# First in-projection and the memory's keys and values as three products of split parts, residual loaded a second time

## The reference, cut to what matters

```python
h  = rmsnorm(x, norm_attn)
z  = h @ w_in                       # 2048 -> some 4200 columns, read by four mixers
o  = concat(mla(z), fox(z), nsa(z), swa(z))
x  = x + group_rmsnorm(o) @ w_out
...
m  = rmsnorm(mem, mem_norm)
k, v = m @ w_xk, m @ w_xv           # 2048 -> 2048 each, used in the second block
```

## Time and profile before

| | before |
|---|---|
| median of 3 runs | 3607.71 us (3600.49 to 3613.07) |
| the profiled execution, its own time | 3600.61 us |
| its span in the trace | 3598.5 us |
| PE busy | 3231.2 us, 90% |
| PEld busy | 2423.2 us |
| DVE busy | 1803.0 us |
| ACT busy | 1125.7 us |
| mean granted clock | 0.970 |
| the first stage (to the first product of `w_out`) | 0 to 700.5 us of the span |

### The profile page before, as it was taken

One profiled execution on the slowest core, in us unless ns is written; L12 is line 12 of the kernel. 1 busy time (PEld: TensorE's weight loads), 2 busy tenths in 40 slices (PEclk: granted clock), 3 DMA queues, 4 the chain that ended last, 5 costly groups with the idle time before them and its releaser, 6 DMA issues.

```text
span 3598.5 us, 41404 instructions
## 1 busy us (share of the span) xinstructions
PE 3231.2 (90%) x17284; PEld 2423.2 (67%) x17284; DVE 1803.0 (50%) x2793; ACT 1125.7 (31%) x2177; POOL 306.2 (9%) x284
## 2 busy tenths in 40 slices
PE   7999999899999999979998899898998768777776
PEld 6667875599999999978897899644443223232222
DVE  1212122265555555665666646555555556655554
ACT  1212122235343434346554434222222222222221
POOL 0000000000000000000000000122222212221221
PEclk9989899999999999989998999999999999999999
DMA  6433433345555555534444434799999999999997
GB/s 188 158 112 111 148 119 118 120 164 176 181 183 187 178 186 183 180 135 161 156 154 175 153 129 141 318 428 427 427 428 421 428 428 424 428 428 428 429 428 339
DMA packets 98946, 908.76 MB, mean 253 GB/s; under 512 B 10278, under 2 KB 20902, under 8 KB 23624
## 3 DMA queue, kind: packets, MB, share of 16 engines
q0 software_dynamic: 36864, 536.89, 35.1%
q1 hardware_dynamic: 49140, 347.05, 27.4%
q10 hardware_dynamic: 12756, 22.18, 2.2%
HBM read 896.64 MB, written 9.44 MB: 252 GB/s over the span
## 4 chain that ended last, share of the span: by engine, by line
PE 68%; DMA 21%; DVE 6%; ACT 3%; issue 1%; ACTq 0%; DVEq 0%; SPq 0%; POOL 0%; POOLq 0%
PE sums L742 12%; PE sums L743 12%; PE sums L744 12%; DMA area<-in_uv,cst 12%; PE sums L938 9%; PE sums L474 8%; DMA hT<-in_uv,cst 5%; PE sums L493 5%; DMA ringx<-in_uv,cst 3%; PE sums L894 2%; DVE area L1964 1%; PE sums L455 1%; ACT cst L987 1%; PE sums L530 1%; ACT area L987 1%
## 5 line engine op out<-in xcount | busy, mean ns | idle before, releaser
L742 PE MATMUL sums<-xh,wh 128*128 128x256 f32 x2688 | 776.7, 289 | 48.6 <-DVE xl L1720 20.4
L1689 DVE TENSOR_TENSOR wl<-ring,wh 128x1024 fp32r<-128x1024 f32 x480 | 585.2, 1224 | 436.0 <-ACT wh L987 435.1
L743 PE MATMUL sums<-xl,wh 128*128 128x256 f32 x2688 | 766.2, 285 | 0.0
L744 PE MATMUL sums<-xh,wl 128*128 128x256 f32 x2688 | 766.0, 285 | 0.0
L987 ACT ACTIVATE wh<-ring 128x1024 fp32r<-128x1024 f32 x480 | 505.7, 1056 | 507.1 <-PE sums L744 495.4
L742 PEld LDWEIGHTS sums<-xh,wh 128*128 128x128 f32 x2688 | 520.4, 194 | 58.2 <-issue 44.3
L938 PE MATMUL sums<-area,cst 128*128 128x512 f32 x984 | 459.5, 613 | 103.5 <-ACT cst L987 103.3
L743 PEld LDWEIGHTS sums<-xl,wh 128*128 128x128 f32 x2688 | 521.0, 194 | 0.8
L744 PEld LDWEIGHTS sums<-xh,wl 128*128 128x128 f32 x2688 | 520.7, 194 | 0.0
L987 ACT ACTIVATE cst<-cst 128x1 f32<-128x1 f32 (+2 forms) x786 | 234.1, 299 | 914.6 <-DVE cst L1964 852.3
L938 PEld LDWEIGHTS sums<-area,cst 128*128 128x128 f32 x984 | 183.3, 193 | 362.1 <-issue 191.5
(11 more groups left out here) (263 smaller groups left out, 3477.0 us busy)
## 6 DMA issues: line engine op xcount, KB each, us to landing
ring<-in_w_up SPq DMA_DIRECT2D x64, 1024.0 KB, 4.8
ring<-in_w_down SPq DMA_DIRECT2D x64, 1024.0 KB, 4.8
ring<-in_w_in_a SPq DMA_DIRECT2D x53, 1024.0 KB, 4.9
ring<-in_w_out SPq DMA_DIRECT2D x32, 1024.0 KB, 4.8
ring<-in_w_xq SPq DMA_DIRECT2D x16, 1024.0 KB, 4.8
ring<-in_w_xo SPq DMA_DIRECT2D x16, 1024.0 KB, 4.8
ring<-in_w_pq SPq DMA_DIRECT2D x16, 1024.0 KB, 11.4
ringx<-in_w_in_a SPq DMA_DIRECT2D x13, 1024.0 KB, 4.9
```

What stands on the lines that cost most here:

```text
L742: te.matmul(bank[:, 0:T], wh[:, j % 3, x], hi[:, k, :], start=k == 0, stop=False)
L743: te.matmul(bank[:, 0:T], wh[:, j % 3, x], lo[:, k, :], start=False, stop=False)
L744: mm = te.matmul(bank[:, 0:T], wl[:, j % 3, x], hi[:, k, :], start=False, stop=k == 15)
L1689: ve.tensor_tensor(wl[:, j % 3, :], ring[:, load % 3, j % 2 * 1024:j % 2 * 1024 + 1024], wh[:, j % 3, :], ALU.subtract).then_inc(lo_in, 1)
```

## The change

The 66 loads of the first in-projection and of the memory's keys and values move to the front of `PLAN`, the list of loads that are split; `chunks` and `rows` are gone, and `chunks3` and `rows3` do their work. The norm of the input is written over `hT`, and the split of it lies where `hT` and `xn` lie, so the residual is read again (2 MB, on ACTq) when the memory's products are done. The memory is split behind the last product of the in-projection. Loads use three slots instead of six; the small weights of the mixers (`w_uq`, `w_ukv`, `cmp_w1`) have places of their own.

```diff
 def _halves():
-    plan = [("w_out", n) for n in range(16)]
+    plan = [("w_in_a", n) for n in range(13)] + [("w_in_b", 0, q) for q in range(4)]
+    plan += [("w_in_a", n) for n in range(13, 21)] + [("w_in_b", 1, q) for q in range(4)]
+    plan += [("w_in_a", n) for n in range(21, 26)]
+    plan += [("w_xk", n) for n in range(16)] + [("w_xv", part, q) for part in range(4) for q in range(4)]
+    plan += [("w_out", n) for n in range(16)]
...
 # tensor: projections()
-                yield from chunks(8, xn, "attn")
-                yield from rows(xn, "fox")
+                yield from chunks3(8, x1h, x1l, split_ready, "w_in", None, bank1)
+                yield from rows3(x1h, x1l, "w_in", "fox", bank1)
...
-                yield from chunks(16, memT, "mem")
+                yield from chunks3(16, m1h, m1l, split_ready, "mem", None, bank1)
                 for part in range(4):
-                    yield from rows(memT)
+                    yield from rows3(m1h, m1l, "mem", None, bank1)
...
 # scalar: start, memory, end of the stage
+            upper()
+            for k in range(16):
+                on.wait_ge(written, k + 1)
+                act(x1h[:, k, :], hT[:, k, :], ACT.Copy).then_inc(xh_in, 1)
+                if k in (3, 15):
+                    upper()
...
+                on.wait_ge(half_spent, SPENT["swa"])
+                for k in range(16):
+                    on.wait_ge(written, WRITTEN["mem"][0] + k + 1)
+                    act(m1h[:, k, :], memT[:, k, :], ACT.Copy).then_inc(xh_in, 1)
                 yield "+mem_in"
...
-            on.wait_ge(spent, SPENT["mem"])
+            on.wait_ge(half_spent, SPENT["mem"])
+            sc.dma_start(hT[:, :, :], A["xT"]).then_inc(h_back, 16)
             on.wait_ge(written, sum(WRITTEN["nsa"]))
             for j in range(2):
                 on.wait_ge(spill[j], 16 * 12)
-            for _ in range(3):
-                upper()
             split(oT)
...
 # vector: start
-            norm("attn", hT, xn, "norm_attn")
+            for k in range(16):
+                ve.scalar_tensor_tensor(hT[:, k, :], hT[:, k, :], G("norm_attn", k), r, ALU.mult,
+                                        ALU.mult).then_inc(written, 1)
+                if k in (1, 7, 15):
+                    lower()
+                if k % 2 and k > 1:
+                    even_lower("w_in", k - 3, hT, x1h, x1l)
+            even_lower("w_in", 14, hT, x1h, x1l)
...
 # vector: add("w_out"), the eviction
+                    on.wait_ge(h_back, 16)
                     ve.tensor_tensor(hT[:, n, :], banks[(TAKEN[stage] + n) % 3][:, 0:T], hT[:, n, :],
                                      ALU.add).then_inc(off_v, off.one())
...
 # gpsimd
+            odd_lower("w_in", hT, x1h, x1l)
+            odd_lower("mem", memT, m1h, m1l)
```

More of the change, by code:

```diff
@@ L294, in program @@
         second.close()
+        halves.close()
         third = ExitStack()
@@ L461, in sum_h, with bank1 @@
                 te.matmul(banks[5][:, 0:T], ones, ssq[:, :], start=True, stop=True).then_inc(ssq_mm, 1)
-            def chunks(n, x, name, part=None):
-                for c in range(n):
[L466 to L478, removed]
+            def bank1():
+                on.wait_ge(evicted, take.n - 2)
+                take.one()
+                return banks[(take.n - 1) % 3]
@@ L479, in chunks @@
                             yield
                     yield "+" + part if part and c == n - 1 else None
[L482 to L497, removed]
@@ L1027, in spill_out, with rows3 @@
                 sc.dma_start(dst, x).then_inc(spill[j % 2], 16)
-            def chunks(ns, part=None):
-                for n in ns:
-                    yield
-                    yield
-                    yield
-                    chunk(n)
-                    yield "+" + part if part and n == ns[-1] else None
-            def rows(evict, part=None):
-                for _ in range(15):
-                    yield
-                for _ in range(4):
-                    loads.one()
-                on.wait_ge(spent, loads.n)
+            def rows3(evict, part=None):
+                for k in range(16):
+                    if k % 2 == 0:
+                        next_half()
+                    if k < 15:
+                        yield
+                on.wait_ge(half_spent, half.n)
@@ L1056, in nsa_rows, with fox_rows @@
+                def fox_rows(t):
+                    act(foxv[:, t, :], banks[off.n % 3][:, :], ACT.Copy).then_inc(evicted, off.one())
+                yield from rows3(fox_rows, "fox")
+                on.wait_ge(prep_mm, 18)
+                yield from chunks3(range(13, 21), chunk)
+                def nsa_rows(t):
+                    bank = banks[off.n % 3]
                     act(vrow[:, t, 0:384], bank[:, 0:384], ACT.Copy)
                     act(gts[:, t, :], bank[:, 384:408], ACT.Sigmoid).then_inc(evicted, off.one())
-                yield from rows(nsa_rows, "nsa")
```

480 lines of the change are left out of this document (207 added, 273 removed).

## The result

| | before | the change |
|---|---|---|
| median | 3604.1 us of 4 runs (3600.3 to 3613.1) | 3547.6 us of 4 runs (3547.2 to 3548.9) |
| ratio, 95% interval | | 0.984 (0.982 to 0.986) |
| the profiled execution, its span | 3598.5 us | 3545.2 us |
| first product of `w_out` | 700.5 us | 647.3 us |

The changed kernel is 1.6% faster. The spans differ by 53.3 us, and so do the starts of `w_out` (700.54 - 647.27 = 53.3): all of it was won in the first stage, and the rest moved as it stood.

A forecast was written before the change was run, and what follows sets the result against it. The first stage was taken as bound by PE. Products (-81.2) and pauses, less the stage's end, summed to -49 us; from a median of 3607.7 that gave 3558 us, range 3530 to 3588.

The forecast's parts named there:

- The products, -81.2: First stage: three split-part products replace each fp32 one, saving 48.5 us at 256 columns and 32.7 at 512.
- The rule of four passes: Skill page's claim: fp32 takes four passes, so three cost 75%, saving 114 us instead of 81; chance 0.03.
- Start, +11.4: Input's split and first `lower` delay PE: chunk 0 ready later, 5.6 us late instead of 5.8 early; bounds 8 and 14.
- First scores of fox, +4: PE's wait for an ACT-DVE chain grows: less covering work, an `upper` and a `lower` possibly inside; bounds 1 and 5.
- Norms, +7: Norms of mla, fox and memory: 4.8 us PE idle while DVE's norm delays `lower`, plus 2; bounds 2 and 10.
- Split of the memory, +4: After the in-projection, PE waits 3.5 us for copies, then the third half's `upper` and `lower`; bounds 2 and 8.
- Compression and last norms, +2: Compression, scores' softmax, last norms: DVE leaves `lower` some 14 us, but PE has few projection products there; bounds 0 and 5.
- Heads, +8: Attention heads: PE takes 6.4 us a head, the ACT-DVE loop 5.7; +8 us in all, bounds 0 and 67.
- The row of 0.55 us a half: Later row blocks: PE waited 8.8 us for `wl` over 16 halves; used as the heads' upper bound, 67 us.
- Loads, 0: First stage's weight loads: requested over 13 us before `upper` needs them, longest landing 12.3 us, so no cost.
- End of the stage, -4.2: Before `w_out`: three `upper` and three `lower` done earlier, about 1 us remains; the residual's load stays hidden.
- The two rivals on the heads: ACT-DVE relay binds heads, 3573 to 3597 us, chance 0.18; or waits in every half make it slower, 3618, chance 0.04.

The follow-up runs named there:

- The two kernels on the start: Against the change: one puts the third `lower` behind the split's last two subtractions, 3544.02 us; the other gives DVE all 16 split subtractions, POOL none, 3543.96 us.

## Why the prediction was right, and where its terms were not

I forecast 3558 us (3530 to 3588) and faster with 0.93; it is 3547.6. The sum was -49 us; between the two profiled executions it is -53.3. The rest of the difference is the 7.1 us by which the median before lay above its profiled execution and which I added: the change's median lies 0.1 us above its own, and the median before is 3604.1 with the later run.

- **The products, -81.2: measured -83 to -85**, of which the memory's are 39.8 by the kernel with them in fp32. The step was right and 2 to 4 us small: I gave every product of 256 columns 0.1198 us, and those of the in-projection took 0.113 to 0.118. The rule of four passes, which gave -114, is not borne out.
- **The pauses.** My terms for them come to +32.2 (11.4 + 4 + 7 + 4 + 2 + 8 - 4.2). PE's idle grew by 18.3 and the cost of the low clock by 13.6 (or some 11.5 by its own products), together 30 to 32. That the sums agree is luck: the terms were mis-sized in both directions, and I had no term for the clock but a sentence in the memory's split.
- **Start, +11.4: about 14.4**, just over my bound of 14. Chunk 4 was evicted at 67.67 us, where the rate alone gives 59.04 - 5.8 = 53.2. I had the waits about right (7.9 us more idle ahead of and between the first products), but not the 16 us more at the low clock that came with them. The two kernels on the start show both the third `lower` (3.9 us with the clock) and POOL's share (2.0) in it.
- **First scores of fox, +4: +0.3**, under my bound of 1. PE waited 3.8 us where it had 3.5. I had an `upper` and a `lower` inside the chain; the `upper` began beside it on ACT at 198.54 us and the `lower` behind its last link, at 200.66.
- **Norms, +7: +6.2, of it 4.9 the wait behind the memory's norm.** This was forecast as 4.8 us of idle with this mechanism, and the kernel with two `lower` inside the norm shows it.
- **Split of the memory, +4: about 2**, with waits of 1.3 and 0.6 us. The first was for a part of `m1l` and the second for ACT's work on `area`; the wait that I had forecast, for the `lower` of the third half, did not come.
- **Compression and last norms, +2: about 1** of idle.
- **Heads, +8: about 2.** The 6.4 us from turn to turn were right, and the step "it fits under 6.4 with 0.7 us left" was too tight. PE's idle over the late heads grew from 0.7 to 2.2 us, and the kernel with 1.2 us more of DVE for each half lost only 6.5 us there. The row of 0.55 us a half, on which two rivals stood, was of long pieces of work and does not carry over to short ones.
- **Loads, 0: right.** No wait of PE or ACT in the stage was on a weight.
- **End of the stage, -4.2: 0.** "In the change those are done earlier" was right, and the three `lower` left the chain. What failed is that I took the store's 2.03 us as given and asked only what the residual's load does to DVE. With three slots a weight load is issued the moment the last `lower` is done, beside the store; holding both loads back gave the 3.8 us.

The two rivals on the heads (3573 to 3597, and slower than before) needed 0.2 to 0.55 us of wait in each of 122 halves. Even with DVE's work on a half doubled it is 0.15 us a half over the whole stage (20 us over 132), so they were far off.

## What to carry to other kernels

When products get cheaper, price the new pauses twice: as idle, and as the low clock that follows them near the start and around small products. Here it was 18 and 12 to 14 us of some 84 won. When a removed piece of work was what ended a chain, look at what shares the DMA engines with the next link, on every queue: a load asked for as soon as a slot is free can land on the one store that all engines wait for, and moving it by 5 us is free. And a price of lateness taken from long pieces of work is a poor bound for short ones; one kernel that adds work to the suspected engine shows the slack better, if PE's own work is compared beside its waits.

## What the runs showed of the hardware that was not expected

Products of 128x256 in the reduced format cost 0.113, 0.118 or 0.120 us at full clock. The same instructions on the same tiles ran at 0.1133 in one kernel and at 0.1178 in another, whose PE program is the same, for a whole uninterrupted stretch; which of the tiles moves counts too. For small edits this is noise of the size of the gain: a stretch of 24 us is 1 us longer at the higher price. The some 11,000 products of this kind in the later stages all cost 0.120, and the step to 0.113 would be 70 us there; what rule decides was not found, and whether those stages can have it was not tried. Two DVE multiplications took 1.35 us beside POOL's subtractions and 0.87 without. The second of two stores of 256 KB took 2.03 us alone, 5.26 beside a 1 MB load that another queue had been given 2 us earlier, and 6.20 with a 2 MB load behind it on its own queue as well.
